# Attention pipelines of a two-block transformer: each unit's transposes two steps behind its scores, instead of three

## The chip, the cores and the metric

The kernel runs on one core of a Trainium2 chip. The metric is the device time of one execution in microseconds; where several executions are timed, their median counts. Every time below comes from one profiled execution or from the timed ones, as said beside it.

## The reference

The program computes two blocks in a row on a sequence of 512 tokens with 1024 channels, in float32. The first block has a sliding-window attention, an RWKV-7 time mix and a gated feed-forward part. The second has two layers, each a mixer and a gated feed-forward part. Four attentions make up the two mixers; three of them are softmax attentions, and these are what the change touches:

```python
# layer 0 ("even"): Fox attention and differential attention, both causal, 512 x 512
s = einsum('bqhd,bkhd->bhqk', qb, k) * scale + (cb[..., :, None] - c[..., None, :])
p = softmax(where(qpos[:, None] >= kpos[None, :], s, -inf)); out = einsum('bhqk,bkhd->bqhd', p, v)
...
p1 = softmax(where(mask, s1, -inf)); p2 = softmax(where(mask, s2, -inf))
p = p1 - lam * p2; out = einsum('bhqk,bkhd->bqhd', p, v)          # v is 128 wide
# layer 1 ("odd"): attention over each query's top 128 keys, as a mask, then stick-breaking attention
s = where(valid, einsum(q_abs, c_sel) + einsum(q_rope, kr_sel), -inf) * scale
p = softmax(s); out = einsum('bqhk,bqkr->bqhr', p, c_sel)
```

## The kernel before

The kernel is a row of stages. Each stage is one block with a program of its own for each engine: TensorE (PE), VectorE (DVE), ScalarE (ACT), GpSimd (POOL) and the DMA queue's engine (SP). Each engine takes its program in the order in which it is written, and the engines meet at semaphores only. A stage begins when the one before has ended on all engines. No planner is in between: the order of the code is the order on the engine.

The function `attend_pairs` is one such stage, and is called twice: by `even_mixer` with 32 units of work and by `odd_mixer` with 16. A unit is one pair of score maps for one block of 128 queries against w keys, where w is 128, 256, 384 or 512, as the attention is causal. In the even layer, units of the Fox attention (two heads, even-numbered here) and of the differential attention (the two maps of one head, odd-numbered) take turns, so that the widths run 128, 128, 256, 256, 384, 384, 512, 512, four times over. In the odd layer the widths run 128, 256, 384, 512, four times over. A differential unit is called `wide` in the code, as its values are 128 wide: its two maps are joined into one on DVE, and only that one is transposed.

A unit u goes through these stations:

- PE: two score matmuls (L1137) into two PSUM banks. Two pairs of banks take turns. For Fox units a matmul with the causal wall comes ahead (L1135).
- DVE: the reduction at L1175 adds the bias or mask, writes the scores to `sm` and their negated maximum to `mx`.
- ACT: two exponentials (L1210) from `sm` into `ex`, with their sum. `ex` has four buffers; exp(u) waits until unit u - 4 is transposed.
- DVE: the reciprocal of the two sums (L1182), and for a wide unit the product with lambda (L1185).
- POOL: multiplies the map or maps by their reciprocal (its instruction is at L1120; a wide unit has one map scaled here, the others two).
- DVE, wide units only: the join at L1192.
- PE: the transposes (L1146), one for each 128 x 128 block. They wait until unit u - 1's transposed maps have been copied out of PSUM.
- The copy of the transposed maps out of PSUM: by DVE (L1199), for a wide unit by ACT (L1218).
- PE: the value matmuls (L1157), and ACT's copy of the result (L1222).

All engines' programs are loops over the same step i. At step i PE issues the scores of unit i, the transposes of unit i - LATE and the values of unit i - LAST. DVE issues the reduction of unit i, the reciprocal of unit i - 1, the join of unit i - 2 and the copy of unit i - LATE. ACT issues the exponentials of unit i, the copy of unit i - LATE if that is wide, and the result's copy of unit i - LAST. Before the change LATE is 3 and LAST is 4.

Of the kernel before, what the change touches and what calls it, by code (L numbers as in the profile page):

```python
# [130 lines left out]
def _program(nc, a, out, whole):  # L131
# [951 lines left out]
    def attend_pairs(units, turned=None):  # L1083


        U = len(units)
        LATE, LAST = 3, 4
        wide = [len(values[0]) == 1 for _, _, _, _, _, values, _ in units]
        nth = [sum(wide[x] == wide[u] for x in range(u)) for u in range(U)]
        with ExitStack() as ctx:  # L1090
# [985 lines left out]
    def even_mixer(cosT, sinT, oT, forget):  # L2076
        lam_init = 0.8 - 0.6 * math.exp(-0.3 * 0)
        with ExitStack() as ctx:
# [4 lines left out]
            with ExitStack() as fx:  # L2083
                aq, ak, av = (sb(fx, n, [P, 4, S]) for n in ("aq", "ak", "av"))
                vta = sb(fx, "vta", [P, NT, 4, P])
                with ExitStack() as pr:
                    af = sb(pr, "af", [P, S])
                    dsts = [af[:, :]] + [t[:, m, :] for t in (av, aq, ak, bv, bq, bk) for m in range(4)]

                    project(25, lambda m: dsts[m],  # L2090
                            lead=Post(pr, forget, "norm_ffn_post", ("attn_norm", 0), [vta[:, t, :, :].rearrange("p m n -> p (m n)") for t in range(2)]),
                            side=EvenSide(pr, af, av, bv, {m: dsts[m] for m in range(17, 25)}, vta, vtb[:, :, :, :], forget, mask,
                                          lam[:, :], lam_init, cosT, sinT))
                close_feed()
                ob = bv
                units = []
                for p in range(NH // 2):
                    for n in range(NT):
                        w = (n + 1) * P
                        units.append(([(aq[g:g + HD, p, n * P:w], ak[g:g + HD, p, 0:w]) for g in (0, HD)], w,  # L2100
                                      [forget[:, 2 * p, 0:w], forget[:, 2 * p + 1, 0:w]], mask[:, S - P:S], None,
                                      [[vta[:, b, p, 0:HD], vta[:, b, p, HD:P]] for b in range(n + 1)], oT[:, p, n * P:w]))
                for h in range(4):
                    for n in range(NT):
                        w = (n + 1) * P
                        units.append(([(bq[p0:p0 + HD, h, n * P:w], bk[p0:p0 + HD, h, 0:w]) for p0 in (0, HD)], w,
                                      [mask[:, S - w:S]] * 2, None, lam[:, 0:1], [[vtb[:, b, h, :]] for b in range(n + 1)], ob[:, h, n * P:w]))
                units = [x for two in zip(units[:4 * NT], units[4 * NT:]) for x in two]
                attend_pairs(units, [av[:, 2 * i:2 * i + 2, :].rearrange("p a b -> p (a b)") for i in range(2)])
# [144 lines left out]
    def odd_mixer(cosT, sinT, oT):  # L2254
        with ExitStack() as ctx:
            sq_, sk_, sv_ = (sb(ctx, n, [P, 4, S]) for n in ("sq", "sk", "sv"))
            bar, after = sb(ctx, "bar", [P, 2 * P]), sb(ctx, "after", [P, P])
            with ExitStack() as ds:
# [47 lines left out]
                for p in range(NH // 2):  # L2306
                    for n in range(NT):
                        w = (n + 1) * P
                        units.append(([(cq[g:g + HD, p, n * P:w], dk[g:g + HD, p, 0:w]) for g in (0, HD)], w,
                                      [future[:, :] if n == 0 else keep[:, n - 1, 0:w]] * 2, None, None,  # L2310
                                      [[dv[:, b, p, 0:HD], dv[:, b, p, HD:P]] for b in range(n + 1)], oT[:, p, n * P:w]))
                attend_pairs(units)
            stick_breaking(sq_, sk_, sv_, bar, after, oT)

# [243 lines left out]
```

## Time and profile before

| what | us |
|---|---|
| median of 3 timed executions | 2338.84 |
| lowest, highest of them | 2334.21, 2342.34 |
| the profiled execution's own time | 2336.04 |
| its span in the trace | 2334.2 |
| PE busy in the span | 2190.0 (94%) |
| DVE busy | 1218.5 (52%) |
| POOL busy | 988.2 (42%) |
| ACT busy | 834.7 (36%) |

The span runs from the first to the last instruction of the trace; the profiled execution's own time is 1.8 us longer and holds what lies around it. Busy times are averages over stages with different limits, so that they tell nothing of a stage of their own: the two calls of `attend_pairs` lie at 1143 to 1230 us and at 1805 to 1850 us of the span.

### The profile page before, as it was taken

The numbers are of one execution on the slowest core, as the hardware profiler recorded it, in microseconds if no ns is written. First come the engines' busy times: TensorE is split into PE (matmuls) and PEld (weight loads), VectorE is DVE, ScalarE is ACT, GpSimd is POOL, SyncE is SP. The second block draws the span as 40 slices with busy tenths as digits, with TensorE's granted clock in tenths as the row PEclk, the third lists the DMA queues.
The fourth block names the chain that finished last, engine by engine and source line by source line (L and its number), as shares of the span: only waits on it lengthen the run. The fifth ranks groups of instructions, "written<-read, shape, count | busy, mean of one in ns | idle before, by whom it ended". The sixth has DMA issues, their size and how long they took to land. (4 is left out here: it accounts for less than half of the span.)

```text
span 2334.2 us, 35182 instructions
## 1 busy us (share of the span) xinstructions
PE 2190.0 (94%) x13241; PEld 1757.2 (75%) x13241; DVE 1218.5 (52%) x1873; ACT 834.7 (36%) x1322; POOL 988.2 (42%) x515
## 2 busy tenths in 40 slices
PE   6995998799999999899888999999999899999998
PEld 4673986688888888777657888888776558888887
DVE  3336534777814772332663577731298633777601
ACT  3443222433313332332353333332233554333322
POOL 5230211344443444366562444444465514444442
PEclk8997999899999999899899999999999999999999
DMA  4220001233332333233101333333332003333332
GB/s 133 55 68 20 4 26 38 81 90 90 108 100 81 100 98 104 81 82 82 46 1 55 91 90 101 96 89 98 92 97 73 1 10 99 90 90 99 88 101 90
DMA packets 347228, 177.23 MB, mean 76 GB/s; under 512 B 20851, under 2 KB 344302, under 8 KB 347118
## 3 DMA queue, kind: packets, MB, share of 16 engines
q1 hardware_dynamic: 346620, 175.60, 26.1%
q8 instruction: 75, 1.23, 0.2%
q14 instruction: 35, 0.29, 0.0%
q10 hardware_dynamic: 210, 0.08, 0.0%
q0 software_dynamic: 288, 0.03, 0.0%
HBM read 173.57 MB, written 2.11 MB: 75 GB/s over the span
## 5 line engine op out<-in xcount | busy, mean ns | idle before, releaser
L313 POOL TENSOR_TENSOR wlo<-raw,whi 128x1024 fp32r<-128x1024 f32 (+3 forms) x347 | 795.1, 2295 | 1069.6 <-ACT whi L847 570.1
L326 PE MATMUL banks<-xhi,whi 128*128 128x512 f32 x1680 | 664.8, 396 | 5.7 <-DVE cb L1033 3.2
L328 PE MATMUL banks<-xhi,wlo 128*128 128x512 f32 x1680 | 655.2, 390 | 0.0
L327 PE MATMUL banks<-xlo,whi 128*128 128x512 f32 x1680 | 654.9, 390 | 0.0
L326 PEld LDWEIGHTS banks<-xhi,whi 128*128 128x128 f32 x1680 | 316.1, 188 | 81.6 <-issue 11.6
L327 PEld LDWEIGHTS banks<-xlo,whi 128*128 128x128 f32 x1680 | 316.2, 188 | 67.5 <-issue 3.4
L328 PEld LDWEIGHTS banks<-xhi,wlo 128*128 128x128 f32 x1680 | 316.0, 188 | 66.8
L955 ACT ACTIVATE cb<-banks,conv 128x512 f32<-128x512 f32 x152 | 117.8, 778 | 444.1 <-DVE banks L1022 444.1
L847 ACT ACTIVATE whi<-raw 128x1024 fp32r<-128x1024 f32 (+1 forms) x205 | 200.4, 987 | 136.4 <-DMA raw<-in_ffn_w_out_dram 61.4
L326 PE MATMUL banks<-ghi,whi 128*128 128x512 f32 x608 | 236.6, 389 | 0.3 <-DVE glo L1043 0.3
L327 PE MATMUL banks<-glo,whi 128*128 128x512 f32 x608 | 236.5, 389 | 0.0
L328 PE MATMUL banks<-ghi,wlo 128*128 128x512 f32 x608 | 236.5, 389 | 0.0
L1022 DVE TENSOR_TENSOR banks<-banks,rs 128x512 f32<-128x512 f32 x152 | 106.0, 699 | 159.3 <-PE banks L328 136.9
L1041 DVE CAST ghi<-gv 128x512 f32 (+1 forms) x76 | 168.3, 2214 | 9.0
L309 ACT ACTIVATE whi<-raw 128x1024 fp32r<-128x1024 f32 (+3 forms) x142 | 137.4, 972 | 48.0 <-PE banks L328 26.8
L326 PEld LDWEIGHTS banks<-ghi,whi 128*128 128x128 f32 x608 | 114.1, 188 | 24.4 <-DVE glo L1043 0.7
L327 PEld LDWEIGHTS banks<-glo,whi 128*128 128x128 f32 x608 | 114.1, 188 | 23.8
L328 PEld LDWEIGHTS banks<-ghi,wlo 128*128 128x128 f32 x608 | 114.1, 188 | 23.5
L1033 DVE SCALAR_TENSOR_TENSOR cb<-banks,conv,cb 128x510 f32<-128x510 f32 x152 | 113.8, 748 | 19.6 <-DVE cb L1031 3.0
L1031 DVE SCALAR_TENSOR_TENSOR cb<-banks,conv,cb 128x511 f32<-128x511 f32 x152 | 112.6, 741 | 4.9 <-ACT cb L955 4.9
L1066 DVE TENSOR_TENSOR xT<-banks,xT 128x512 f32 (+1 forms) x16 | 11.1, 691 | 191.8 <-PE banks L328 191.8
L1120 POOL TENSOR_SCALAR ex<-ex,mx 128x128 f32<-128x128 f32 (+3 forms) x80 | 87.9, 1113 | 49.0 <-DVE mx L1182 34.5
(460 smaller groups left out, 2606.6 us busy)
## 6 DMA issues: line engine op xcount, KB each, us to landing
raw<-in_ffn_w_in_dram SPq DMA_DIRECT2D x88, 512.0 KB, 3.8
raw<-in_w_ffn_up_dram SPq DMA_DIRECT2D x64, 512.0 KB, 4.0
raw<-in_w_ffn_down_dram SPq DMA_DIRECT2D x32, 512.0 KB, 3.6
raw<-in_ev_w_in_dram SPq DMA_DIRECT2D x25, 512.0 KB, 3.9
raw<-in_ffn_w_out_dram SPq DMA_DIRECT2D x32, 384.0 KB, 3.5
raw<-in_ffn_w_out_dram SPq DMA_DIRECT2D x32, 320.0 KB, 3.2
raw<-in_od_w_in_dram SPq DMA_DIRECT2D x20, 512.0 KB, 3.6
raw<-in_w_in_dram SPq DMA_DIRECT2D x16, 512.0 KB, 3.7
```

What stands on the lines that cost most here:

```text
L309: w_hi.by(act.activation(whi[s % CUT][:, 0:n, :], raw[s % RAW][:, 0:n, :], ACT.Copy))
L313: return pool.tensor_tensor(wlo[c][:, 0:n, :], raw[b][:, 0:n, :], whi[c][:, 0:n, :].bitcast(F32), ALU.subtract)
L326: pe.matmul(acc, whi[b][:, k, :], hi(k), start=first and k == 0, stop=False)
L327: pe.matmul(acc, whi[b][:, k, :], lo(k), start=False, stop=False)
L328: mm = pe.matmul(acc, wlo[b][:, k, :], hi(k), start=False, stop=last and k == n - 1)
L847: act.activation(whi[s % CUT][:, 0:n, :], raw[s % RAW][:, 0:n, :], ACT.Copy).then_inc(w_hi.h, 1)
L955: act.activation(cb[j][:, :], bank[j][:, :], ACT.Identity, scale=conv[:, 2, bass.ds(c, 1)], bias=conv[:, 3, bass.ds(c, 1)])\
L1022: dve.tensor_tensor(bank[j % 4][:, :], bank[j % 4][:, :], rs, ALU.mult).then_inc(scaled.h, 1)
L1031: chain(dve.scalar_tensor_tensor(cb[j][:, 1:S], bank[j][:, 0:S - 1], conv[:, 1, bass.ds(c, 1)], cb[j][:, 1:S], ALU.mult, ALU.add))
L1033: dve.scalar_tensor_tensor(cb[j][:, 2:S], bank[j][:, 0:S - 2], conv[:, 0, bass.ds(c, 1)], cb[j][:, 2:S], ALU.mult, ALU.add).then_inc(conve ...
L1041: dve.tensor_copy(ghi[:, i * 2 + q, :], gv[q][:, :]).then_inc(upper.h, 1)
L1120: ins = pool.tensor_scalar(ex[u % 4][:, g, 0:w], ex[u % 4][:, g, 0:w], mx[u % 4][:, 2, g:g + 1], None, ALU.mult)
```

## The change

The two constants of `attend_pairs` become one smaller. Nothing else is changed: no instruction is added, dropped or altered, and every wait is on the same event of the same unit as before.

```diff
         U = len(units)
-        LATE, LAST = 3, 4
+        LATE, LAST = 2, 3
         wide = [len(values[0]) == 1 for _, _, _, _, _, values, _ in units]
```

The first place is PE's program in the odd layer's attention. dk and cq are keys and queries, so that L1137 is a unit's scores; ex is the exponentiated map, so that L1146 is a unit's transposes; pt is the transposed map and dv the values. Before:

```order
L1146 MATMUL banks<-cst,ex_433 128x128 x8
L1157 MATMUL banks<-pt_434,dv 64x128 x6
L1137 MATMUL banks<-dk,cq 128x512 x2
L1146 MATMUL banks<-cst,ex_430 128x128 x2
L1157 MATMUL banks<-pt_435,dv 64x128 x8
L1137 MATMUL banks<-dk,cq 128x128 x2
```

And now, from the same transposes to the same 512-wide scores:

```order
L1146 MATMUL banks<-cst,ex_433 128x128 x8
L1157 MATMUL banks<-pt_434,dv 64x128 x6
L1137 MATMUL banks<-dk,cq 128x384 x2
L1146 MATMUL banks<-cst,ex_430 128x128 x2
L1157 MATMUL banks<-pt_435,dv 64x128 x8
L1137 MATMUL banks<-dk,cq 128x512 x2
L1146 MATMUL banks<-cst,ex_431 128x128 x4
```

Between the eight transposes of unit 3 and the scores of unit 7 stood one group of value matmuls; now there stand the scores of unit 6, the transposes of unit 4 and another group of value matmuls as well.

The second place is PE's program in the even layer's attention, around the 512-wide scores of a wide unit. bk and bq are its keys and queries, vtb its values; ak, aq and vta belong to the Fox units. Before:

```order
L1137 MATMUL banks<-bk,bq 128x512 x2
L1146 MATMUL banks<-cst,ex_293 128x128 x6
L1157 MATMUL banks<-av,vtb 128x128 x2
L1135 MATMUL banks<-wall,eye 128x128 x2
L1137 MATMUL banks<-ak,aq 128x128 x2
L1146 MATMUL banks<-cst,ex_294 128x128 x3
L1157 MATMUL banks<-av,vta 64x128 x6
```

And now:

```order
L1137 MATMUL banks<-bk,bq 128x512 x2
L1146 MATMUL banks<-cst,ex_294 128x128 x3
L1157 MATMUL banks<-av,vta 64x128 x6
L1135 MATMUL banks<-wall,eye 128x128 x2
L1137 MATMUL banks<-ak,aq 128x128 x2
L1146 MATMUL banks<-cst,ex_295 128x128 x8
L1157 MATMUL banks<-av,vtb 128x128 x3
```

The three transposes of the joined map ex_294 stood behind the next unit's scores, and stand now directly behind the scores of the 512-wide unit; those of the Fox unit before it have moved ahead of these rows.

The third place is DVE's program in the even layer, at the 128-wide scores that follow a 512-wide Fox unit, as one piece of the difference:

```order
 L1182 RECIPROCAL mx_300<-mx_300 128x2
 L1185 TENSOR_SCALAR mx_300<-mx_300,lam 128x1
+L1199 COPY av<-banks 128x1024
 L1175 ISA sm_292,mx_298<-banks,mask 128x128
 L1175 ISA mx_298 128x1
```

```order
 L1182 RECIPROCAL mx_297<-mx_297 128x2
 L1192 SCALAR_TENSOR_TENSOR ex_296<-ex_296,mx_300 128x512
-L1199 COPY av<-banks 128x1024
 L1175 ISA sm_291,mx_299<-banks,f 128x256
```

The copy of a Fox unit's transposed maps stood behind the join of a wide unit, and stands now one step earlier, between the reciprocal and the reduction of a wide unit's scores. The join has not moved.

## Rows read from the trace of the kernel before

**Rows 1.** The page: its head, and POOL's group of the normalising scale.
```profile
span 2334.2 us, 35182 instructions
...
L1120 POOL TENSOR_SCALAR ex<-ex,mx 128x128 f32<-128x128 f32 (+3 forms) x80 | 87.9, 1113 | 49.0 <-DVE mx L1182 34.5
```

**Rows 2.** Windows, each engine's busy us (x instructions), granted clock, DMA share, GB/s.
```profile
1143.00:1229.80 86.80, 70.77 (x520) 47.23 (x520) 55.03 (x209) 50.09 (x177) 53.93 (x48) 0.93 0.00 1
1160.66:1180.74 20.08, 16.35 (x131) 11.00 (x130) 13.79 (x53) 12.19 (x45) 13.53 (x13) 1.00 0.00 1
...
1820.14:1830.22 10.08, 8.71 (x78) 5.41 (x76) 7.04 (x27) 5.57 (x20) 8.50 (x8) 1.00 0.00 0
```

**Rows 3.** Waits in 1160.66 to 1180.74: us, times, longest.
```profile
PEld banks L1146 <- POOL ex L1120: 4.3, 3, 2.1
...
PE banks L1146 <- ACT av L1218: 2.6, 2, 1.3
```

**Rows 4.** Timeline of the odd attention: start us, busy us, engine, what [idle before].
```profile
1814.17 0.92 PE L1137 MATMUL banks<-dk,cq 64*128 64x384 f32 x4
...
1815.86 1.09 PE L1146 MATMUL banks<-cst,ex 128*128 128x128 f32 x8 [0.77 <-POOL ex L1120]
...
1816.88 0.88 PE L1157 MATMUL banks<-pt,dv 128*64 128x128 f32 x12
...
1817.69 1.13 PE L1137 MATMUL banks<-dk,cq 64*128 64x512 f32 x4
...
1818.75 0.44 PE L1146 MATMUL banks<-cst,ex 128*128 128x128 f32 x2
1818.86 0.69 DVE L1175 CUSTOM_DVE_ANT_0 sm<-banks,keep 128x512 f32<-128x512 f32 x1 [0.65 <-PE banks L1137]
...
1819.11 1.09 PE L1157 MATMUL banks<-pt,dv 128*64 128x128 f32 x16
...
1820.09 0.16 DVE L1182 RECIPROCAL mx<-mx 128x2 f32<-128x2 f32 x1
...
1820.14 0.49 PE L1137 MATMUL banks<-dk,cq 64*128 64x128 f32 x4
...
1820.35 8.50 POOL L1120 TENSOR_SCALAR ex<-ex,mx 128x384 f32<-128x384 f32 x8 [1.59 <-DVE mx L1182]
...
1825.94 1.09 PE L1146 MATMUL banks<-cst,ex 128*128 128x128 f32 x8 [0.77 <-POOL ex L1120]
```

**Rows 5.** Windows of line L1175 alone, DVE's busy us (x instructions).
```profile
1160.66:1180.74 20.08, 7.27 (x32) 1.00 0.00 1
```

**Rows 6.** Windows of line L1192 alone, DVE's busy us (x instructions).
```profile
1160.66:1180.74 20.08, 2.25 (x4) 1.00 0.00 1
```

**Rows 7.** Timeline of the even attention, PE and DVE around a 512-wide score.
```profile
1174.90 1.13 PE L1137 MATMUL banks<-ak,aq 64*128 64x512 f32 x4
...
1175.96 0.44 PE L1146 MATMUL banks<-cst,ex 128*128 128x128 f32 x2
...
1177.50 0.21 DVE L1185 TENSOR_SCALAR mx<-mx,lam 128x1 f32<-128x1 f32 x1
...
1179.35 0.84 PE L1146 MATMUL banks<-cst,ex 128*128 128x128 f32 x6 [1.31 <-ACT av L1218]
...
1180.03 0.61 PE L1157 MATMUL banks<-av,vtb 128*128 128x128 f32 x4
...
1180.23 0.96 DVE L1199 COPY av<-banks 128x768 f32<-128x768 f32 x1 [0.24 <-PE banks L1146]
```

**Rows 8.** Timeline, the first matmul of the even attention.
```profile
1143.07 0.69 PE L1135 MATMUL banks<-wall,eye 128*128 128x128 f32 x2 [2.90 <-DVE wall L1167]
```

**Rows 9.** Windows behind that matmul.
```profile
1143.00:1155.00 12.00, 11.62 (x47) 7.29 (x49) 6.99 (x36) 7.22 (x26) 5.38 (x7) 0.51 0.01 2
```

**Rows 10.** Timeline, a matmul of the first layer behind a like gap.
```profile
70.87 0.63 PE L1860 MATMUL banks<-cst,ex 128*128 128x128 f32 x4 [2.91 <-DVE ex L1981]
```

**Rows 11.** Windows behind that one.
```profile
71.00:74.00 3.00, 3.00 (x16) 2.56 (x16) 0.00 (x0) 1.55 (x2) 0.84 (x1) 1.00 0.05 14
```

## The prediction, written before the changed kernel was run

> **What bounds the kernel now.** I read the page first, for where the changed lines stand. The normalising scale, the one POOL instruction that only `attend_pairs` has, occurs 80 times [rows 1]: 48 in the even layer's attention and 32 in the odd layer's. Then windows, to get the size of the two stages. The even one fills 1143 to 1229.8 us, 32 units in four groups of eight whose widths run 128, 128, 256, 256, 384, 384, 512, 512; one group takes 20.08 us, with PE busy 16.35, DVE 13.79 and POOL 13.53 [rows 2]. The odd one has 16 units in four groups of widths 128, 256, 384, 512, each 10.08 us long, with PE busy 8.71 and POOL 8.50 [rows 2]. No engine is full in either. So both stages are held by a loop of dependences that runs through several engines, and only some 4 x 20.1 + 4 x 10.1 = 121 us of the 2334 us span [rows 1, 2] can react to the change at all. The reader should look there for a loop, not for a busiest engine.
>
> I write sc(u), tr(u), val(u) for the score matmuls, the transposes and the value matmuls of unit u, and red(u), rec(u) for DVE's score reduction (L1175) and reciprocal (L1182). The waits view of one even group says what PE waits for: its weight loads 4.3 us for POOL's scale, its transposes 2.6 us for ACT [rows 3]. The timeline of the odd stage shows the loop whole [rows 4]. With units 0 to 3 in the first group and 4 to 7 in the second: tr(3) starts at 1815.86, val(2) 1.02 later, sc(7) 0.81 later, red(7) 1.17 later, rec(6) 1.23 later, at 1820.09. rec(6) stands behind red(7) in DVE's program, and POOL's scale(6) and scale(7) start only with it; 5.85 us after rec(6) begins, tr(7) starts, at 1825.94. The sum is 1.02 + 0.81 + 1.17 + 1.23 + 5.85 = 10.08, just the period. The loop closes over four units, and contains 3.0 us of PE work that POOL has to sit out: POOL idles 1.59 us in each round [rows 4].
>
> **The change, part by part.** Nothing is added or removed. tr moves from three to two steps behind sc, and val from four to three, on PE; DVE's copies and ACT's copies of the same unit move with them. No DMA moves, since SP has nothing in these stages.
>
> *Odd stage.* PE takes its matmuls in the order of the program. Before, sc(7) came one step after tr(3): between them only val(2). Now tr(3) is in step 5 and sc(7) in step 7. Between them stand val(2), sc(6), tr(4), val(3). So three terms enter the loop: sc(6), 0.85 us (busy 0.92, less the 0.07 by which a 1.13 us pair is cut short by its follower at 1818.75), tr(4), 0.36, and val(3), 1.03 [rows 4]. The rest of the loop is unchanged, since rec(6) still waits behind red(7) and scale(7) behind scale(6). New period: 10.08 + 0.85 + 0.36 + 1.03 = 12.32, that is 2.24 us more for four units. tr(3) to tr(15) is three such periods: 6.7 us. In the first group the loop isn't closed yet, but sc(3) now stands behind tr(0), which waits for POOL's first scale; I estimate half a group's loss and a little, 1.3 us. The end is the same: tr(15), val(14), val(15), last copy. The step that is saved there is one in which PE would only wait for scale(15). Odd stage: +8.0 us.
>
> *Even stage.* Here odd-numbered units are wide (two score maps, joined by DVE at L1192). The join of u stands on DVE two steps behind red(u), before and after, so it comes behind red(u+2). Before, tr(u) for that unit stood a step later, behind sc(u+3): PE had work while DVE reduced and joined. Now tr(u) stands directly behind sc(u+2) and waits for the join, and everything on PE waits behind it. So in each of a group's four steps with a wide unit, PE's work no longer lies beside DVE's: sc, red, join and tr are in a row. Per group that makes: all PE work, 16.35 [rows 2]; half of the reductions, 7.27 / 2 = 3.6 [rows 5]; the four joins, 2.25 [rows 6]; eight hand-offs between the engines, four at about 0.05 and four at about 0.1 (rec(6) at 1820.09 plus 0.16 busy to POOL at 1820.35 [rows 4]), 0.6. Sum 22.8.
>
> That takes DVE as free when each score arrives. It isn't, as DVE's copy of the other kind of unit is now put ahead of the wide unit's reduction. At the 512-wide pair: from the start of sc(6) DVE needs 1.17 + 1.23 [rows 4], then reciprocal about 0.2 and lambda product 0.21, then the 768-wide copy, 0.96 [rows 7], in sum 3.8; PE offers sc(7) after 1.06 (1174.90 to 1175.96), 0.68 (1179.35 to 1180.03) and 0.37 of transposes and values, plus 1.17, in sum 3.3 [rows 7, 4]. DVE is 0.5 late. The same comparison at the 384 and 128 pairs gives 0.5 and 0.3. And POOL needs about 3.3 for two halves of 512 behind rec(6) while PE is back at tr(6) in 3.0: 0.5 late. In sum 1.8, so 24.6; some loose ends of 0.05 make it 24.8 to 25.1. I take 24.9, against 20.08: +4.8 per group, +14.5 for three. In the first group the same waits stand in front of a PE at half clock [rows 9], and walking its seven steps in the same way puts sc(7) about 5 us later; I take 5.0. The end costs nothing: POOL's last scales and the last join set it in both kernels. Even stage: +19.5 us.
>
> *Sum.* 8.0 + 19.5 = 27.5 us. Against the profiled execution's own 2336.0 us this is 2363.5; that execution is 2.8 us under the median of the three runs, 2338.8, so I predict 2338.8 + 27.5 = 2366.
>
> Bounds from below: without DVE being late and without POOL's lateness a group costs 22.8, +2.7; four of them 11 us. In the odd stage the smallest loop that must exist is tr(u), val(u-1), sc(u+3), red(u+3), rec(u+2), scale(u+2), which closes over two units. For odd u its two rounds hold, by widths, about 2.1 + 4.0 of PE, reduction and reciprocal and 5.0 of POOL, 11.3 with hand-offs, +1.2 per group, 5 in all. So 16 us: 2355. From above: the first group and hand-offs could be worth 3 us more, and the clock (below) far more.
>
> **Rivals.** *The clock.* In the new order PE stands still in each step with a wide unit, longest behind sc of a 512-wide one: 1.17 - 1.06 + 0.5 + 1.23 + 0.1 + 0.6 + 0.1, about 2.6 us. The trace has gaps of that size with both outcomes: after 2.90 us idle the even stage starts at a granted clock of 0.50, that is 1.2 GHz [rows 8, 9]; after 2.91 us idle in the first layer it stays at 1.00, 2.4 GHz [rows 10, 11]. What PE did ahead of them differs, so a gap alone doesn't decide it. If it falls once in each of the seven later groups and stays low as long as at the stage's start, 12 us [rows 9], then some 8 us of PE work in each fall takes up to twice as long; I take half as long again, 4 us, of which a part hides behind POOL, say 3 us of loss: 7 x 3 = 21, time 2387. The Trainium skill, "TensorE: Matmul & The Clock Gate", Part 1: The HAM clock gate, says that the half rate is the default state and that activity releases it; by that rule a busy share that sinks speaks for this rival. PE's share sinks from 0.81 to 0.66 in the even stage. The trace bears it out only in part, as rows 10 and 11 show.
>
> *No change.* If PE's idle time before (3.7 us a group in the even stage, 1.4 in the odd) could take in the new waits, 2339. It speaks against it that the odd loop has no slack: its terms add up to the period exactly.
>
> *Faster.* Mechanism: PE's idle time in the even stage goes, because the transposes of narrow units no longer meet ACT's copy queued behind an exponential (2.6 us a group [rows 3]), and one step of some 2.5 us is saved at the end of each stage. Price: 4 x 2.6 + 2 x 2.5 = 15 us, time 2323. It decides if the scale of unit u is ready when PE comes to it two steps behind; in the odd stage it already isn't at three steps (0.77 us idle at 1815.86 and 1825.94 [rows 4]).
>
> **How the numbers follow.** The forecast's case, PE in a row with DVE and POOL at full clock, 0.72, its own range 2355 to 2375. The clock falling, 0.20. No change, 0.05. Faster, 0.03. The range 2354 to 2386 holds the first case and most of the second. A measurement of this kernel tells about 0.3%, 7 us, from no change; both slower cases lie beyond that: slower 0.92, same 0.05, faster 0.03.
>
> **What would show it.** In the odd stage, 12.3 us between tr of successive 512-wide units, with sc(6), tr(4), val(3) between; POOL's idle time in each round near 3.8 instead of 1.59. In the even stage, about 25 us per group; PE's transposes waiting for DVE's join (L1192), where before they waited for ACT; ACT's waits gone; no group of waits new on SP. Wrong would be: an even group under 22 us (then PE isn't in a row with DVE), a granted clock under 0.9 behind 1160 us in the even stage, or any stage outside these two that changes its length.

## The result: slower by 2.4%, and twice as much as predicted

The changed kernel takes 2392.97 us (median of 4, 2390.80 to 2393.70), the kernel before 2338.05 (median of 4, 2334.21 to 2342.34). The ratio is 1.0243, 95% interval 1.0230 to 1.0257 (the two medians by themselves give 1.0235; further down, too, a ratio and its medians can differ by about 0.001). The forecast was 2366 with a range up to 2386: the direction is right, the size is not.

The page of the changed kernel, against [rows 1]:

```profile
span 2391.9 us, 35182 instructions
...
L1120 POOL TENSOR_SCALAR ex<-ex,mx 128x128 f32<-128x128 f32 (+3 forms) x80 | 89.0, 1123 | 97.0 <-DVE mx L1182 58.3
```

The reader sees that POOL does the same work in nearly the same time (89.0 us busy, 87.9 before) but stands idle in front of it for 97.0 us, where it was 49.0. POOL's work hasn't become dearer; POOL waits more.

The windows of the changed kernel say where. Each line gives the stretch and its length, the busy us of PE, of PE's weight loads, of DVE, ACT and POOL, the granted clock, the DMA share and GB/s. In this order: the even stage, the part of it from the scores of the third to the wall of the seventh unit of a group, the 19.96 us from there to the third unit's wall in the next group, the odd stage, and four units of it.

```profile
1145.39:1273.90 128.51, 101.12 (x520) 66.40 (x520) 54.20 (x208) 52.14 (x178) 54.82 (x48) 0.69 0.00 1
1181.05:1191.45 10.40, 7.37 (x50) 4.38 (x49) 5.84 (x26) 5.74 (x22) 4.92 (x6) 0.97 0.00 0
1191.45:1211.41 19.96, 16.61 (x81) 11.43 (x79) 7.63 (x26) 6.77 (x22) 8.89 (x7) 0.59 0.00 1
1851.79:1908.72 56.93, 41.49 (x304) 26.56 (x305) 28.66 (x96) 23.58 (x82) 34.22 (x32) 0.85 0.00 1
1871.49:1883.83 12.34, 8.74 (x77) 5.42 (x77) 7.19 (x27) 5.57 (x20) 8.56 (x8) 1.00 0.00 1
```

The stages of before, from the first matmul of each to the first work of the stage behind it:

```profile
1143.07:1230.10 87.03, 70.76 (x520) 47.23 (x520) 55.02 (x208) 50.07 (x178) 53.93 (x48) 0.93 0.00 1
1804.87:1850.24 45.37, 34.81 (x304) 21.63 (x305) 28.24 (x96) 23.63 (x82) 34.00 (x32) 1.00 0.01 1
```

So the even stage has grown by 41.5 us and the odd one by 11.6, in sum 53.0; the two spans differ by 57.7, and the rest is within what two executions of one kernel differ by elsewhere. The granted clock of the even stage has fallen from 0.93 to 0.69, that of the odd one from 1.00 to 0.85, and DVE, ACT and POOL are as busy as before to a few per cent, while PE's busy time has risen by 30 us on the same 520 matmul records.

The waits view of the changed kernel's even stage (us, times, longest) shows what PE now waits for:

```profile
PEld banks L1146 <- DVE ex L1192: 35.2, 16, 3.3
PE banks L1146 <- DVE ex L1192: 24.7, 16, 2.0
```

All sixteen transposes of wide units wait for DVE's join. The wait for ACT's copy, 2.6 us a group in [rows 3], has gone. PE's timeline of one group shows both the waits and the clock:

```profile
1180.68 0.44 PE L1135 MATMUL banks<-wall,eye 128*128 128x128 f32 x2
...
1187.51 0.92 PE L1137 MATMUL banks<-bk,bq 64*128 64x384 f32 x4
1190.25 0.44 PE L1146 MATMUL banks<-cst,ex 128*128 128x128 f32 x2 [1.82 <-DVE ex L1192]
1190.61 0.91 PE L1157 MATMUL banks<-av,vta 128*64 128x128 f32 x8
1191.45 0.69 PE L1135 MATMUL banks<-wall,eye 128*128 128x128 f32 x2
1192.07 2.08 PE L1137 MATMUL banks<-ak,aq 64*128 64x512 f32 x4
...
1196.41 1.75 PE L1137 MATMUL banks<-bk,bq 64*128 64x512 f32 x4
1200.17 0.55 PE L1146 MATMUL banks<-cst,ex 128*128 128x128 f32 x3 [2.01 <-DVE ex L1192]
1200.65 1.14 PE L1157 MATMUL banks<-av,vta 128*64 128x128 f32 x12
1201.72 0.69 PE L1135 MATMUL banks<-wall,eye 128*128 128x128 f32 x2
```

Behind the gap of 1.82 us the clock falls: the 512-wide scores take 2.08 us, 1.13 in [rows 7]. It comes back within the next ones (1.75 us), so that the transposes behind the gap of 2.01 us begin at the upper level (0.55 us), and then it falls a second time: the pair at L1135 takes 0.69 us, 0.44 at the upper level (first row). Both falls come back at the same places in each of the three groups that follow the first, 30.7 us apart; in the first group, which starts at the lower level, there is only the one behind 2.01 us.

### The profile page after: what moved, and what is told of

Same layout as the page of the kernel before. It is cut to its first block and busy times, and to the rows that moved or that the text cites. A ratio compares the mean times of both kernels' runs of the same rounds, so it can differ in the third digit from the quotient of the medians.

```text
span 2391.9 us, 35182 instructions
## 1 busy us (share of the span) xinstructions
PE 2231.3 (93%) x13241; PEld 1783.4 (75%) x13241; DVE 1217.5 (51%) x1873; ACT 837.2 (35%) x1322; POOL 990.3 (41%) x515
```

## The experiments

Two theories stood at first. Mine: two causes add up, the loop of dependences that closes one step sooner (27.5 us, as predicted) and a fall of PE's clock in the gaps that it makes. The rival: the waits themselves cost it all, and the slower matmuls lie in time in which PE would have waited anyway.

**Each stage by itself.** The edits, each in a kernel of its own, in `attend_pairs`, where only the even stage's call has `turned`:

```diff
-        LATE, LAST = 2, 3
+        LATE, LAST = (2, 3) if turned else (3, 4)      # the even stage alone
+        LATE, LAST = (3, 4) if turned else (2, 3)      # the odd stage alone
```

> The new lags (2 and 3) in the even layer's attention alone; the odd layer's keeps 3 and 4. The traces put +41.5 us of the loss between the start of the even attention and the start of the norm behind it, and 11.6 us in the odd attention. Theory 1 (each attention loses by itself, a loop of dependences plus a fall of TensorE's clock inside the stage): 2338 + 42 to 44 = 2380 to 2382 us, the clock low in the second half of each group of eight units as in the changed kernel. Rival (something outside the two stages, a clock or a prefetch that is carried over, makes part of it): under 2375 or over 2387.

> The new lags in the odd layer's attention alone. Theory 1: 2338 + 8 (the loop alone) to 11.6 (with the clock falling twice, as in the changed kernel), so 2346 to 2350 us; and this and the run with the even stage alone add up to the whole loss of 55 us. Rival (interplay): the two losses add up to less than 50 or more than 60.

Measured: 2381.81 us with the even stage alone (ratio 1.0199, 1.0182 to 1.0216) and 2347.64 with the odd one alone (1.0047, 1.0031 to 1.0064), against 2337.65. That is 44.2 and 10.0 us, in sum 54.2 of 54.9. The traces give 128.3 us for the even stage and 57.1 for the odd one, as in the changed kernel, and the other stage of each is as before (45.4 and 86.5). The losses are local and add up.

**PE kept at work in its gaps.** This kernel adds matmuls whose result nobody reads. The two waits ahead of the transposes change places, so that the idle matmuls stand between them; the transposes still wait for both:

```diff
                     if 0 <= u < U:
-                        wait_normed(pe, u)
                         if u >= 1:
                             wait_taken(pe, u - 1)
+                        for _ in range((((1, 1, 2, 3)[i // 2 % 4] if i % 2 else 0) if turned else (3, 1, 0, 1)[i % 4]) if i < U else 0):
+                            pe.matmul(bank[5], ident, xT[:, 0, :], start=True, stop=True)
+                        wait_normed(pe, u)
```

> The changed kernel, and in the time in which PE waits for a join or a scale it does matmuls whose result nobody reads (512 columns, into the PSUM bank that is free just then; 1, 1, 2 and 3 for the four widths in the even stage, 3, 1, 0, 1 in the odd one), each about 0.55 us at full clock, in sum less than the wait. Theory 1 (20 to 28 us of the 55 are the clock, the rest the loop): the granted clock stays at 1.00 behind the first microseconds, a group of eight takes 25 us in place of 30.7, four units of the odd stage 12.3 to 12.4, and the time falls to about 2338 + 28 = 2366 us, though work was added. Rival (the loop itself costs it all, and the clock is a symptom): no faster than 2393.

Measured: 2369.21 us (1.0137, 1.0120 to 1.0154). The kernel does more work and is 23.8 us faster than the changed one. Windows of its even stage and of one group:

```profile
1144.63:1249.80 105.17, 97.25 (x574) 56.37 (x574) 53.44 (x208) 52.98 (x177) 54.69 (x48) 0.96 0.00 1
1167.82:1192.80 24.98, 23.78 (x145) 13.79 (x144) 13.28 (x52) 12.99 (x45) 13.79 (x13) 1.00 0.00 1
```

At a clock of 1.00 a group takes 24.98 us; the prediction had worked out 24.9. The even stage is 18.1 us over before (19.5 predicted). So of its 41.5 us at least 23.3 were the clock's, and the rival theory is out. It is "at least", as the filling costs something itself. From a wall pair to the transposes behind the 384-wide scores of a wide unit this kernel takes 9.98 us:

```profile
1173.55 0.44 PE L1135 MATMUL banks<-wall,eye 128*128 128x128 f32 x2
...
1183.53 0.38 PE L1148 MATMUL banks<-cst,ex 128*128 128x128 f32 x2
```

The changed kernel takes 9.57 us there, also at the upper level (1180.68 to 1190.25, above): the two idle matmuls end 0.4 us behind the join. The loop alone is therefore worth about 24.6 us per group, by this estimate, and not 24.98. In the odd stage this run says nothing, for my idle matmuls were too long: a 512-wide one takes 0.95 us, not 0.55, and three of them, 2.84 us, filled a gap of 1.9, so that the stage took 58.0 us.

**The same with shorter filling in the odd stage**, one matmul of 0.95 us per four units:

```diff
-... if turned else (3, 1, 0, 1)[i % 4]) if i < U else 0):
+... if turned else (1, 0, 0, 0)[i % 4]) if i < U else 0):
```

> The changed kernel with idle matmuls, in the even stage as in the first such run, in the odd one a single one of 0.95 us where PE waits longest (1.9 us, behind the 128-wide scores). In the first run the odd stage's idle matmuls were too long for their gaps (2.84 us in one of 1.9) and stretched four units to 13.05 us. Theory (the loop is worth 8.0 us in the odd stage, the clock the other 3.6): the clock stays up, four units take 12.3 us, the stage 53.4 us in place of 56.9, and the time is 2338 + 18 + 8 = 2364 us. Rival (the 3.6 us aren't the clock's): odd stage 56 us or more, 2367 to 2370.

Measured: 2365.57 us (1.0124, 1.0102 to 1.0146), beside the 2366 that the prediction had for a full clock. Against its own runs of before, 2335.03, it is 30.5 us, where 26 were expected; the two stages of its trace account for 27.3 (104.7 and 55.0 us). Windows of its odd stage and of four units of it:

```profile
1825.04:1880.07 55.03, 43.36 (x311) 26.31 (x311) 28.93 (x97) 23.68 (x82) 34.15 (x32) 0.88 0.00 1
1850.31:1862.70 12.39, 9.81 (x79) 5.72 (x79) 7.23 (x24) 5.56 (x21) 8.55 (x9) 1.00 0.01 1
```

Four units take 12.39 us at full clock. The stage is 1.6 us longer than the 53.4 expected; its mean clock of 0.88 says that it still ran at the low level for part of its first and last units. The loop's share in the odd stage is therefore at most 9.7 us of 11.6. That it is 8.0, as forecast, no run shows; only its 12.3 us per four units are measured.

**One gap filled.** Which gap makes the clock fall? This kernel fills only the one of 1.8 us, in the even stage; the two waits change places as in the first such run:

```diff
+                        for _ in range(2 if turned and i % 8 == 5 else 0):
+                            pe.matmul(bank[5], ident, xT[:, 0, :], start=True, stop=True)
```

> The changed kernel with idle matmuls in one place of each group of the even stage only: behind the 384-wide scores of a wide unit (two matmuls of 512 columns, about 1.1 us of the 1.8 us for which PE waits there). In the changed kernel's trace the clock falls directly behind that gap in three groups of three, and not behind the longer one of 2.0 us that follows. Theory A (the fall comes from how little PE did in the whole stretch from there on back, so that this one gap decides): the clock stays up, even stage -20 us, about 2371 us. Theory B (any gap of that size will do, and the next one, 2.0 us behind the 512-wide scores, takes its place): the fall comes a few us later in each group, 2383 to 2392 us.

Measured: 2379.54 us (1.0188, 1.0174 to 1.0203), even stage 115.1 us. PE's timeline:

```profile
1164.83 0.52 PE L1148 MATMUL banks<-cst,ex 128*128 128x128 f32 x3 [2.19 <-DVE ex L1194]
1165.28 0.88 PE L1159 MATMUL banks<-av,vta 128*64 128x128 f32 x12
...
1181.22 1.98 PE L1144 MATMUL banks<-xT,cst 128*128 128x512 f32 x4 [0.41 <-DVE av L1201]
...
1189.93 0.52 PE L1148 MATMUL banks<-cst,ex 128*128 128x128 f32 x3 [2.19 <-DVE ex L1194]
1190.38 1.06 PE L1159 MATMUL banks<-av,vta 128*64 128x128 f32 x12
1191.37 0.69 PE L1135 MATMUL banks<-wall,eye 128*128 128x128 f32 x2
```

The clock stays up through the filled gap and falls behind the next one (the pair at L1135 takes 0.69 us; at full clock it is 0.42 to 0.44). What was expected rested on a misreading: the changed kernel's clock falls behind the gap of 2.0 us as well, as its timeline above shows. So the filling took away the first of two falls and left the second, and the even stage is 13.4 us shorter. The time lies between the ranges of the two theories, 3.5 us under B's, and the run settles neither of them: B is right that filling one gap doesn't keep the clock up, but no fall has moved there from elsewhere. It shows one thing more. In the first group the same gap of 2.19 us is followed by no fall: the twelve value matmuls behind it take 0.88 us, and 1.06 in the group behind, where the clock falls in them.

**One part of the change alone**: the transposes two steps behind the scores, as changed, the values four, as before.

```diff
-        LATE, LAST = 2, 3
+        LATE, LAST = 2, 4
```

> One part of the change alone: transposes two steps behind the scores, as changed, but the values four steps, as before. Theory (it is the transposes' place that closes the loop one step sooner; the values are only work that lies in it): nearly all of the loss remains, the loop of the odd stage losing 0.4 us per four units for smaller value groups in it, the even one holding sc, red, join and tr in a row as before; the clock falls too: 2385 to 2393 us. Rival (the values' place matters as much): under 2370.

Measured: 2386.85 us (1.0218, 1.0194 to 1.0243), 51.8 of the 54.9 us. The even stage takes 123.0 us and the odd one 57.1. It is the transposes' place that costs; the values' place alone was not run. For the odd stage my detail was wrong: four units take 12.56 us (tr at 1869.24 and 1881.80), not the 11.9 that I had from the smaller value groups. PE waits 0.64 us per round for a copy of DVE there, which my sum did not have.

**One step more instead of one less**, in the kernel before:

```diff
-        LATE, LAST = 3, 4
+        LATE, LAST = 4, 5
```

> The kernel before with the lags one larger instead of smaller: transposes four steps behind the scores, values five. Theory 1 (the number of steps around which the loop closes sets the period until an engine is full): the odd stage comes to POOL's own time, 8.6 us per four units in place of 10.1, minus 5 us in all; the even one from 20.1 towards 18 us per group, minus 6 to 8; so about 2326 us, less one step of 2 us more at each end, 2328. Rival (the exponentials of unit i wait for the transposes of unit i - 4, now in the same step, and take back what is gained): 2335 to 2345.

Measured: 2336.40 us against 2337.65 (0.9996, 0.9986 to 1.0006): no difference. That lies in the rival's range. Windows of the two stages:

```profile
1142.47:1234.50 92.03, 80.45 (x520) 53.29 (x520) 54.73 (x208) 50.23 (x178) 54.44 (x48) 0.84 0.00 1
1808.28:1849.16 40.88, 34.38 (x304) 21.63 (x305) 28.00 (x97) 23.62 (x82) 34.01 (x32) 1.00 0.01 2
```

The odd stage gains 4.5 us, as its loop promised. The even stage loses 5.0, its clock 0.84. PE's timeline has the place:

```profile
1161.65 0.85 PE L1146 MATMUL banks<-cst,ex 128*128 128x128 f32 x6 [1.58 <-ACT av L1218]
...
1181.35 1.32 PE L1146 MATMUL banks<-cst,ex 128*128 128x128 f32 x6 [1.58 <-ACT av L1218]
1182.45 1.06 PE L1157 MATMUL banks<-av,vtb 128*128 128x128 f32 x4
1183.44 0.80 PE L1137 MATMUL banks<-bk,bq 64*128 64x128 f32 x4
```

There is PE's wait for ACT's copy, 1.58 us, and behind it matmuls at half clock (0.80 for scores that take 0.49). A group earlier the same wait is followed by transposes at the upper level (0.85 us). My theory's 2328 failed in the even stage, which I had expected to gain as well. The rival's wait is there too: ACT's exponentials wait 10.1 us for transposes in the even stage, and not at all before. This run alone doesn't separate it from ACT's copy.

**ACT's copy ahead of the exponentials**, with lags 3 and 4, then with 4 and 5 in the odd stage only, then with 4 and 5 in both. The edit common to the three, in ACT's program:

```diff
                 for i in range(U + LAST):
+                    u = i - LATE
+                    if 0 <= u < U and wide[u]:
+                        act.wait_ge(flipped.h, u + 1)
+                        if u >= 2:
+                            act.wait_ge(weighed.h, u - 1)
+                        act.activation(*copied(u), ACT.Copy).then_inc(wtaken.h, 1)
                     if i < U:
...
-                    u = i - LATE
-                    if 0 <= u < U and wide[u]:
-                        ...
```

> The kernel before (lags 3 and 4), with ACT's copy of a wide unit's transposed map ahead of the exponentials of the same step, no longer behind them. In the trace of before PE's transposes wait 9.0 us in the even stage for this copy, which stands behind exponentials that are themselves waiting for DVE. Theory: the wait goes, 5 to 9 us, 2329 to 2333 us. Rival: the wait was only the last of several that end together, and the step's length is DVE's: under 3 us, 2335 to 2338.

> The kernel before with the same move of ACT's copy, and lags of 4 and 5 in the odd layer's attention only. In the run with the deeper lags in both stages the odd one took 4.5 us less than before and the even one 5 us more. Theory: the gain in the odd stage stands by itself, so 4 to 5 us under the run that moves the copy alone: 2325 to 2329 us.

> Lags of 4 and 5 in both stages, and ACT's copy moved ahead of the exponentials. Theory: what made the even stage slower at the deeper lags was this copy standing behind exponentials (PE gaps of 1.6 us behind which the clock fell); with it moved, the even stage is no longer than with lags 3 and 4: 2322 to 2328 us. Rival: the exponentials' own wait for the transposes four units back holds the stage: 2329 to 2335.

Measured, against 2336.67 us: 2331.50 (0.9981, 0.9972 to 0.9990), 2328.27 (0.9967, 0.9956 to 0.9979) and 2329.87 (0.9967, 0.9955 to 0.9978). The first is as expected. The second lies in its range, though it is 3.2 us under the first and not 4 to 5. The third missed its 2322 to 2328 and lies in the rival's range. The copy's wait is gone from the even stage, which takes 83.3 us with lags of 3 and 4 (87.0 before, or 86.5 in the run that left it alone, whose stage starts at the upper level as this one does). That is 3.2 to 3.7 us and not the 9.0 of that wait: PE waits longer for DVE's copies instead, 9.4 us where it was 5.2. The odd stage takes 40.9 us in both of the others. With the deeper lag and the copy moved the even stage takes 84.8, where it was 92.0 with the copy in its old place: the deeper lag cost 5.0 us with the copy in its old place and 1.5 with it moved, so that the copy was most of it, but deeper is no gain there even so. The windows of the second of the three:

```profile
1144.71:1227.90 83.19, 71.33 (x520) 48.07 (x520) 54.02 (x208) 51.29 (x177) 53.87 (x48) 0.92 0.00 1
1802.86:1843.74 40.88, 34.38 (x304) 21.63 (x305) 28.00 (x96) 23.60 (x82) 33.92 (x32) 1.00 0.01 2
```

It beats both kernels, the one before by 0.33%.

## Why the prediction was wrong, by its own steps

**Where the loss lies: right.** Only the two stages changed, 53.0 of 57.7 us of the spans. They are 132 us long and not the 121 of the prediction, which left out their first groups and ends; 11 us of the loss lie there in the even stage.

**The loop of the odd stage: right.** Predicted 12.32 us per four units; 12.34 at full clock in the changed kernel (the last of its windows above). POOL's idle time in that round was forecast near 3.8 us and is 3.7:

```profile
POOL ex L1120 <- DVE mx L1182: 3.7, 2, 2.8
```

**PE in a row with DVE in the even stage: right.** 24.9 us per group predicted, 24.98 in the run with the gaps filled. That the two agree to 0.1 is partly luck: 0.4 us of the 24.98 is the filling's, and 0.3 us of the 24.9 are the sum's "loose ends", which rest on no row. The sum without them is 24.6, and so is the estimate above for the loop alone. Its small terms for DVE and POOL being late (1.8 us) were not measured one by one. The first group was set at +5.0; it came to +8.1 in the changed kernel (scores of unit 0 to unit 7: 1146.01 to 1167.26, 13.2 us before), of which the filled run keeps 3.7. That the end costs nothing holds at full clock only: with the gaps filled it is 0.3 us shorter than before, in the changed kernel 3.0 us longer.

**The choice between the cases: wrong.** The step that failed is the one in "How the numbers follow" that gave full clock 0.72 and the falling clock 0.20, and so made 2366 the prediction. The changed kernel shows the fall in all four groups, and with it the prediction's own sign of being wrong, a granted clock under 0.9 behind 1160 us. I had put the two gaps of 2.9 us in [rows 8, 10] against each other and concluded that a gap alone doesn't decide. That is so, but it is no reason to hold the fall for unlikely in a stage in which PE waits 1.2 to 2.0 us four times in each group, and in which its share was forecast to sink to two thirds. (The longest of these gaps was forecast at 2.6 us and is 2.0.) The rule of the Trainium skill that the prediction cited ("TensorE: Matmul & The Clock Gate", Part 1: The HAM clock gate: the half rate is the default, and activity releases it) spoke for the fall, and the trace agrees: the granted clock is 0.59 over the 19.96 us that begin behind the gap of 1.82 us, in which PE is busy 16.61.

**The price of the fall: undersized, and the range with it.** The rival gave 3 us of loss in each of the seven later groups, 9 in the even stage and 12 in the odd one, in sum 21, 2387; the range ended at 2386. Measured in the even stage, changed kernel against filled one: 15.7 us over the three periods from one group's 512-wide scores to the next's (90.6 against 3 x 24.98; 5.7 in the full ones), and 4.4 in the first group and 3.3 at the end, which the rival had at nothing; that makes up the 23.3. In the odd stage it is 1.9 us by the filled run, and 3.6 if the loop is worth the 8.0 forecast. The term that was mis-sized is that some 8 us of PE work in each fall take half as long again, 4 us, of which 1 is hidden in waits. In a full group of the changed kernel the clock falls twice, and PE is busy 8.0 us more than before:

```profile
1211.78:1242.51 30.73, 24.35 (x132) 16.12 (x131) 13.47 (x52) 12.76 (x45) 13.82 (x12) 0.72 0.01 2
```

Against 16.35 us in [rows 2] that is 8.0, of which 5.7 or a little more lengthen the group and some 2 are hidden. So a part is hidden, as the rival said; the amount that isn't was twice its figure in the even stage, where PE's work is on the path nearly everywhere. In the odd stage PE is busy 6.7 us more (41.49 against 34.81) and 3 to 5 us of it are hidden, as PE waits for POOL there.

**The faster rival: rightly small.** Its mechanism, ACT's wait going, did happen. It was worth 3.2 to 3.7 us of stage when it was had without the shorter lag.

## What to carry to other kernels

In a pipeline written out by hand, a lag is not slack but the number of steps over which a loop of dependences closes: write the loop down with its durations, and see how many steps of in-order work lie in it before a lag is shortened. A sum like that can be right to some 0.3 us per group and still miss the time, if it opens gaps on TensorE: then price the stage at both clock levels, count every fall in a round, and ask for the added PE time how much of it lies in waits (here some 2 of 8 us in the even stage, where PE was on the path, and 3 to 5 of 6.7 in the odd one, where POOL was). Filling the gaps with matmuls that nobody reads is a cheap way to tell the two costs apart.

## What the runs showed of the hardware

The clock of PE fell from its upper to its lower level behind gaps far shorter than the 2.9 us of [rows 8]: 1.82 us after scores in the changed kernel, 2.19 in the run with one gap filled, and 1.58 in the run with the deeper lags, where PE had been busy 17.34 of the 21.55 us ahead, while gaps of 1.3 us in the same stage of the kernel before left it at 1.00 [rows 3, 2]:

```profile
1159.80:1181.35 21.55, 17.34 (x135) 11.42 (x133) 14.95 (x59) 14.03 (x50) 15.32 (x13) 1.00 0.01 2
1181.35:1185.00 3.65, 3.65 (x17) 2.88 (x17) 1.70 (x8) 1.09 (x6) 3.17 (x4) 0.53 0.00 0
```

The length of the gap alone doesn't decide. The same gap had both outcomes in one trace: 1.58 us in the run with the deeper lags (no fall at 1161.65, a fall at 1181.35), 2.19 us in the run with one gap filled, and 1.91 us in the changed kernel's odd stage, where six transposes took 0.87 us behind one and 1.54 behind the next. Behind the gap of 2.90 us at the start of the even stage the first wall pair took 0.69 us in five traces and 0.44 in the seven others, in which the next wall pair, some 1.5 us on, took 0.69. What decides was not settled. A gap may also be filled with work of no use at a net gain: 23.8 us here.
